# 128-row expert items with weight blocks stationary, in a one-core mixture-of-experts encoder

## What is computed

```python
def expert_block(args):                       # one block of up to 128 token rows of one expert
    e, tok, gt = args
    xb = hf[tok]
    g = xb @ w_gate[e] + b_gate[e]            # 1024 x 1024 each
    u = xb @ w_up[e] + b_up[e]
    g = jnp.minimum(g, SWIGLU_LIMIT)          # 7.0
    u = jnp.clip(u, -SWIGLU_LIMIT, SWIGLU_LIMIT)
    act = (u + 1.0) * (g * jax.nn.sigmoid(g * SWIGLU_ALPHA))
    y = act @ w_down[e] + b_down[e]
    return y * gt[:, None]
```

## Time and profile before

| | |
|---|---|
| median of 3 runs | 2243.87 us (2242.58 to 2245.83) |
| the profiled execution | 2242.51 us, its span 2240.7 us |
| granted TensorE clock, mean | 0.988 |
| busy share: TensorE, weight loads, VectorE, ScalarE, GpSimd | 97%, 45%, 29%, 25%, 20% |
| moved by DMA | 499.68 MB, 223 GB/s on average |

### The profile page before, as it was taken

One profiled execution on the slowest core, in us unless ns is written; L12 is line 12 of the kernel. 1 busy time (PEld: TensorE's weight loads), 2 busy tenths in 40 slices (PEclk: granted clock), 3 DMA queues, 4 the chain that ended last, 5 costly groups with the idle time before them and its releaser, 6 DMA issues.

```text
span 2240.7 us, 30792 instructions
## 1 busy us (share of the span) xinstructions
PE 2177.0 (97%) x10323; PEld 1006.9 (45%) x10324; DVE 649.7 (29%) x1915; ACT 564.8 (25%) x1160; POOL 457.1 (20%) x490
## 2 busy tenths in 40 slices
PE   8999999996999999999999899999999999999997
PEld 4444577543444344344434434434443444444443
DVE  2100599255322222221222212312112221222233
ACT  2000588211221222211122221222112221222223
POOL 1014011223121222212121221221122121122222
PEclk9999999997999999999999999999999999999998
DMA  7100200325567977758869795793889967677775
GB/s 265 44 35 0 116 1 1 110 105 199 187 204 288 364 249 239 284 188 316 312 205 365 237 367 192 238 351 121 326 303 381 348 234 277 247 253 262 255 262 188
DMA packets 149336, 499.68 MB, mean 223 GB/s; under 512 B 10265, under 2 KB 34478, under 8 KB 148750
## 3 DMA queue, kind: packets, MB, share of 16 engines
q1 hardware_dynamic: 113632, 443.80, 51.3%
q0 software_dynamic: 33792, 50.35, 10.9%
q10 hardware_dynamic: 1874, 5.02, 0.6%
HBM read 460.84 MB, written 42.50 MB: 225 GB/s over the span
## 4 chain that ended last, share of the span: by engine, by line
PE 94%; DMA 3%; DVE 1%; issue 1%; ACT 0%; POOL 0%; SPq 0%; DVEq 0%; ACTq 0%; POOLq 0%
PE psum L1530 41%; PE psum L1566 14%; PE psum L1264 10%; PE psum L1325 5%; PE psum L1577 4%; PE psum L1348 3%; PE psum L1314 3%; PE psum L1443 2%; PE psum L1538 2%; DMA weights<-in_w_down 2%; PE psum L1524 2%; PE psum L1512 1%; PE psum L1589 1%; PE psum L1601 1%; PE psum L1357 1%; DMA weights<-in_w_up 1%
## 5 line engine op out<-in xcount | busy, mean ns | idle before, releaser
L1530 PE MATMUL psum<-weights,work 128*128 128x512 f32 (+2 forms) x3008 | 968.3, 594 | 0.0
L1530 PEld LDWEIGHTS psum<-weights,work 128*128 128x128 f32 (+2 forms) x3008 | 364.9, 159 | 449.7 <-issue 443.7
L612 POOL DMA_INDIRECT residual_rows<-work x184 | 286.6, 1558 | 444.6 <-ACT work L818 398.2
L1566 PE MATMUL psum<-weights,work 128*128 128x512 f32 x768 | 337.5, 592 | 0.0
L1072 DVE TENSOR_REDUCE work<-psum 128x8 f32 x47 | 8.7, 184 | 790.0 <-PE psum L1457 790.0
L571 POOL DMA_INDIRECT work<-normed_rows,work x48 | 49.3, 1028 | 862.6 <-DVE work L1059 801.9
L1264 PE MATMUL psum<-weights 128*128 128x512 f32 x512 | 220.9, 592 | 1.3 <-DVE weights L890 1.3
L1566 PEld LDWEIGHTS psum<-weights,work 128*128 128x128 f32 x768 | 143.9, 190 | 164.4 <-issue 160.8
L790 ACT ACTIVATE work<-psum 128x256 f32<-128x256 f32 x188 | 71.9, 383 | 386.3 <-PE psum L1530 362.1
L777 ACT ACTIVATE work<-psum 128x512 f32<-128x512 f32 x96 | 57.6, 600 | 435.0 <-PE psum L1443 433.3
L1151 DVE TENSOR_SCALAR work<-psum 128x256 f32<-128x256 f32 x188 | 79.6, 424 | 259.6 <-ACT work L790 252.8
(11 more groups left out here) (213 smaller groups left out, 1669.2 us busy)
## 6 DMA issues: line engine op xcount, KB each, us to landing
weights<-in_w_gate SPq DMA_DIRECT2D x64, 2048.0 KB
weights<-in_w_up SPq DMA_DIRECT2D x64, 2048.0 KB
weights<-in_w_down SPq DMA_DIRECT2D x64, 2048.0 KB, 10.6
weights<-in_w_in SPq DMA_DIRECT2D x8, 768.0 KB, 14.4
residual_rows<-x SPq DMA_DIRECT2D x9, 512.0 KB, 5.4
normed_rows<-work ACTq DMA_DIRECT2D x9, 512.0 KB, 4.8
x<-in_x SPq DMA_DIRECT2D x8, 512.0 KB, 9.7
bias_rows_repeated<-bias_rows SPq DMA_DIRECT2D x4, 1024.0 KB, 9.9
```

The source lines that it names most:

```text
L612: pl.indirect_dma_start(acc_d[:, :], bass.IndirectOffsetOnAxis(dest[:, b:b + 1], 0), yrow[:, b * BLK:(b + 1) * BLK], None, compute_op=ALU. ...
L1530: mm = pe.matmul(out.rearrange("p (m n) -> p m n", m=2), xT[:, k, lo:lo + cols], wgu[:, :, k, blk * BLK:(blk + 1) * BLK], start=False, sto ...
L1566: mm = pe.matmul(bank(4 + h), actT[:, k, :], wdn[:, k, h * HALF:(h + 1) * HALF], start=False, stop=(k == DT - 1))
```

## The change

In 128-row items the sides are exchanged for gate and up: a 128x128 block of the weights is stationary and the 128 token rows move, so the result lies with inner columns on partitions, as the down projection needs it. The transposes and the copies' results are no longer used there: `down_all` takes `hid` itself. The bias products go; VectorE's unit, for every kind of item, adds a bias per partition from a new table `bias_cols` (loaded once, 16 columns an expert; the up half has one added by GpSimd; for the other kinds the table holds zeros, as their bias is still added on TensorE). The column is addressed from registers by the item's kind and expert. The sigmoid now reads the clamped gate from SBUF, and the clamps are in another order. In the 128-row body `hidden` is gone; ScalarE's copies stay and are released by steps on `s_htp` within the gate/up products and the down bias. Two sets of semaphores (`s_x`, `s_res`) become one.

```diff
@@ sync @@
             sp.wait_ge(s_biasp, 1)
+            sp.dma_start(bias_128, t["bias_cols"]).then_inc(s_bcols, 16)
             sp.dma_start(gfin, ...
@@ gpsimd @@
+                if i == 6:
+                    pl.wait_ge(s_biasp, 1)
+                    pl.memset(bias_none, 0.0).then_inc(s_bzero, 1)
...
             gather_rows(1)
+            pl.wait_ge(s_bcols, 16)
+            pl.tensor_scalar(up_cols, up_cols, 1.0, None, ALU.add).then_inc(s_bready, 1)
             pl.wait_ge(s_accin, 16 * (TT + 1))
@@ scalar @@
             def sigmoid(j, b):
-                act.wait_ge(s_gu, UNIT * j + b + 1)
-                act.activation(sig[:, b, :], bank(b, BLK), ACT.Sigmoid, scale=ALPHA).then_inc(s_sig, 1)
+                act.wait_ge(s_gcl, 2 * UNIT * j + (2 * b + 2))
+                act.activation(sig[:, b, :], gact[:, b, :], ACT.Sigmoid, scale=ALPHA).then_inc(s_sig, 1)
@@ vector @@
+            dve.wait_ge(s_bzero, 1)
+            dve.wait_ge(s_bready, 1)
+
+            def own_columns():
+                return (dve.snap(own_kind, min_val=0, max_val=KINDS - 1) * (16 * EXPERTS) +
+                        dve.snap(own_expert, min_val=0, max_val=EXPERTS - 1) * 16)
 
-            def unit(j, b):
+            def unit(j, b, cols):
+                dve.wait_ge(s_gu, UNIT * j + b + 1)
+                for s in range(2):
+                    dve.tensor_scalar(gact[:, b, s * P:(s + 1) * P], bank(b, P, s * P),
+                                      bias_cols[:, bass.ds(cols + (2 * b + s), 1)], LIMIT, ALU.add,
+                                      ALU.min).then_inc(s_gcl, 1)
+                for s in range(2):
+                    dve.tensor_scalar(ucl[:, b, s * P:(s + 1) * P], bank(b, P, BLK + s * P),
+                                      bias_cols[:, bass.ds(cols + (DT + 2 * b + s), 1)], LIMIT + 1.0, ALU.add,
+                                      ALU.min).then_inc(s_ucl, 1)
+                dve.wait_ge(s_gcl, 2 * UNIT * j + (2 * b + 2))
                 dve.wait_ge(s_sig, UNIT * j + b + 1)
-                dve.tensor_scalar(ucl[:, b, :], bank(b, BLK, BLK), LIMIT + 1.0, 1.0 - LIMIT, ALU.min,
-                                  ALU.max).then_inc(s_ucl, 1)
-                dve.tensor_tensor(gact[:, b, :], bank(b, BLK), sig[:, b, :], ALU.mult).then_inc(s_sg, 1)
-                dve.wait_ge(s_ucl, UNIT * j + b + 1)
+                dve.tensor_tensor(gact[:, b, :], gact[:, b, :], sig[:, b, :], ALU.mult).then_inc(s_sg, 1)
+                dve.wait_ge(s_ucl, 2 * UNIT * j + (2 * b + 2))
                 dve.wait_ge(s_sg, UNIT * j + b + 1)
-                dve.scalar_tensor_tensor(hid[:, b, :], gact[:, b, :], ACT_LIMIT, ucl[:, b, :], ALU.min,
+                dve.scalar_tensor_tensor(hid[:, b, :], ucl[:, b, :], 1.0 - LIMIT, gact[:, b, :], ALU.max,
                                          ALU.mult).then_inc(s_hid, 1)
@@ tensor @@
+                def gate_up_128(b, ks):
+                    for k in ks:
+                        for m in range(2):
+                            for s in range(2):
+                                mm = pe.matmul(bank(b, P, m * BLK + s * P), wgu[:, m, k, (2 * b + s) * P:(2 * b + s + 1) * P],
+                                               xT[:, k, :], start=(k == 0 and m + s == 0), stop=(k == DT - 1 and m + s == 2))
+                                if b and k == DT - 1 and m + s == 0:
+                                    mm.then_inc(s_htp, 1)
+                    return mm
...
                 def down_all(b):
-                    pe.wait_ge(s_aTm, UNIT * j + b + 2)
+                    pe.wait_ge(s_hid, UNIT * j + UNIT + b + 1)
...
-                            mm = pe.matmul(bank(4 + h), actT[:, k, :], wdn[:, k, h * HALF:(h + 1) * HALF],
+                            mm = pe.matmul(bank(4 + h), hid[:, b, (k - 2 * b) * P:(k - 2 * b + 1) * P], wdn[:, k, h * HALF:(h + 1) * HALF],
...
                 if tokens == 128:
-                    gate_up_ends(0)
-                    gate_up_ends(1)
-                    hidden(0)
-                    gate_up_ends(2)
-                    hidden(1)
-                    gate_up_ends(3)
+                    for b in range(4):
+                        gate_up_ends(b)
                     next_item()
-                    hidden(2)
                     rows(1)
                     down_bias()
                     down_all(0)
-                    hidden(3)
                     down_all(1).then_inc(s_d03, 1)
```

More of the change, by code:

```diff
@@ L202, in encoder_kernel @@
         bdn = biasp[0:3 * EXPERTS, 2 * D:3 * D]
+        bias_cols = Z[:, 12288:12288 + KINDS * EXPERTS * 16]
+        bias_128 = bias_cols[:, 0:EXPERTS * 16]
+        bias_none = bias_cols[:, EXPERTS * 16:]
+        up_cols = bias_128.rearrange("p (e m f) -> p e m f", m=2, f=DT)[:, :, 1, :]
         xg = Z[:, 0:1024]
@@ L325, in encoder_kernel @@
         s_ucl = sem("up_clamped")
+        s_gcl = sem("gate_clamped")
+        s_bcols = sem("bias_columns_in")
+        s_bzero = sem("bias_columns_cleared")
+        s_bready = sem("bias_columns_ready")
         s_sig = sem("sigmoid_ready")
@@ L1166, in chain @@
                         dve.wait_ge(s_dve, j * PER + (LOOP0 + local[0]))
-                    e1 = dve.value_load(items[0:1, bass.ds(j + 1, 1)], min_val=0, max_val=EXPERTS - 1)
+                    cols = own_columns()
+                    dve.reg_load(own_expert, items[0:1, bass.ds(j + 1, 1)])
+                    dve.reg_load(own_kind, items[0:1, bass.ds(j + (2 * TABLE + 1), 1)])
+                    e1 = dve.snap(own_expert, min_val=0, max_val=EXPERTS - 1)
                     e3 = dve.value_load(items[0:1, bass.ds(j + 3, 1)], min_val=0, max_val=EXPERTS - 1)
-                    kind = dve.value_load(items[0:1, bass.ds(j + (2 * TABLE + 1), 1)], min_val=0, max_val=KINDS - 1)
+                    kind = dve.snap(own_kind, min_val=0, max_val=KINDS - 1)
                     places(chain, j + 1, kind)
@@ L1176, in _ @@
                             index_parts(j + 2)
-                        unit(j, b)
+                        unit(j, b, cols)
                     dve.wait_ge(s_biased, j + 1)
@@ L1194, in _ @@
             dve.sem_inc(s_found, 1)
-            unit(last, 0)
-            unit(last, 1)
+            cols = own_columns()
+            unit(last, 0, cols)
+            unit(last, 1, cols)
             dve.wait_ge(s_added, n_items)
@@ L1201, in _ @@
             dve.sem_inc(s_dest, 1)
-            unit(last, 2)
-            unit(last, 3)
+            unit(last, 2, cols)
+            unit(last, 3, cols)
             dve.wait_ge(s_gfin, 16)
@@ L1517, in gate_up @@
                         return gate_up_32(b, ks)
-                    lo, cols, groups = (0, P, 1) if tokens == 128 else (0, 64, 2) if b < 2 and tokens > 32 else \
-                        (64 if b else 0, 32, 4)
+                    if tokens == 128:
+                        return gate_up_128(b, ks)
+                    lo, cols, groups = (0, 64, 2) if b < 2 else (64, 32, 4)
                     for c in range(groups):
-                        blk = b if tokens == 128 else 2 * c + b if cols == 64 else c
+                        blk = 2 * c + b if cols == 64 else c
                         out = PS[c * cols:(c + 1) * cols, b * HALF:(b + 1) * HALF].rearrange("p (m n) -> p m n", m=2)
@@ L1546, in down_bias @@
                                            start=True, stop=False)
+                            if h == 0:
+                                mm.then_inc(s_htp, 1)
                     if tokens in (64, 96):
@@ L1775 @@
     last = np.concatenate([gain, np.repeat(share.reshape(KINDS, -1), P, 0)], 1).astype(np.float32)
+    bias_cols = np.stack([inputs["b_gate"][0], inputs["b_up"][0]], 1).reshape(EXPERTS, 2, DT, P)
+    bias_cols = bias_cols.transpose(3, 0, 1, 2).reshape(P, EXPERTS * 16)
     arrays, aps = {}, {}
-    for name, a in list(inputs.items()) + [("onehot", onehot), ("edges", edges), ("tables", tables), ("same", same),
+    for name, a in list(inputs.items()) + [("onehot", onehot), ("edges", edges), ("tables", tables), ("same", same), ("bias_cols", bias_cols),
                                            ("last", last)]:
```

19 lines of the change are left out of this document (11 added, 8 removed).

## The result

| | before | after |
|---|---|---|
| median | 2244.70 us (4 runs, 2242.58 to 2245.83) | 2318.35 us (4 runs, 2317.03 to 2320.95) |
| ratio, 95% interval | | 1.0332 (1.0319 to 1.0344) |
| span of the profiled execution | 2240.7 us | 2319.0 us |
| granted TensorE clock, mean | 0.988 | 0.974 |
| busy share: TensorE, weight loads, VectorE | 97%, 45%, 29% | 94%, 60%, 34% |

A forecast was written before the change was run, and what follows sets the result against it. TensorE, 94% of the chain, was taken as the bound; -15.1 + 13.2 + 4.2 + 0.5 - 0.7 = +2.1 us on 2242.5, forecast 2245 us, no change. The range was 2230 to 2272.

The forecast's parts named there:

- The 128-row items on TensorE: 24 items: 42.2 us of bias products and transposes removed, 27.1 added by the exchange at 0.1117 us pitch; 15.1 us less.
- The rival of a pitch that doesn't hold: Gate/up products of 128-row items: 0.118 us a record over long runs, +39 us, 2284; chance 8%.
- VectorE's unit: All 47 items: the unit grows from 1.20 to 2.0 us (1.85 to 2.4), hidden in 128- and 96-row items.
- 32-row items: Choice of next expert comes later behind four longer units: 2.2 us in six of eight items, 13.2 us more.
- 64-row items: Down products start 0.6 us later behind a delayed sigmoid and ScalarE copy; seven items, 4.2 us more.
- The rival of hidden units: Small items hide the longer unit if it stays under 1.35 us: 2227 to 2230, faster; chance 14%.
- The start: Before the first item: bias table lands near 566, VectorE's loop begins near 567 instead of 563; 0.5 us more (0 to 1.5).
- The end: Last item: ScalarE's copy for block 3 no longer waits for the last transposes; 0.7 us less.
- the weighing of the code: Rival that TensorE's longer loop no longer stays loaded: 2253 to 2300, likeliest near 2256, slower; chance 32%.
- the prediction's own sign for it: TensorE's queue: instruction packets after 761 us, with idle time behind a jump that no semaphore explains.
- Eight such places at 1 us are +8: Lower case of refetched loop code: TensorE stalls behind short products of 96- and 32-row items, largely covered by queued products.
- The upper case of the rival: Refetched loop code: sixteen places with two fetches of 2 us, +60, within the code rival's 2253 to 2300.

The follow-up runs named there:

- wait_moved: Changed kernel with VectorE's waits for cleared columns and bias table moved behind the first item's count and index copies; 2314.55 us.
- two_units: Changed kernel with shared 64/96-row code, earlier expert choice, later table wait, and the new VectorE/ScalarE unit only in 128-row items; 2233.57 us, ratio to before 0.9945.
- order_128_last: Changed kernel with TensorE's code for the four kinds laid in the order 32, 64, 96, 128 instead of 32, 128, 64, 96; 2299.18 us.

## Why the prediction was wrong

**The 128-row items on TensorE: right.** The pitch was put at 0.1117 us and is 0.1116; the gain was put at 0.63 us an item and is 0.58 on average. The rival of a pitch that doesn't hold is out, which leaves the row of attention a good witness for runs eight times as long. The rule of the Trainium skill, TensorE: Matmul & The Clock Gate, section Back-to-back issue gap (81 ns a pair where the product alone needs 56), applied as a ratio, would have made it 0.16; the trace disagrees with that use of it.

**VectorE's unit: right in place and size.** It was put at 2.0 us; in a 32-row item of the changed kernel the copies that begin two units in a row start 2.03 us apart:

```profile
856.89 0.60 DVE L1176 TENSOR_SCALAR work<-psum,work 128x128 f32<-128x128 f32 x2
...
858.92 0.60 DVE L1176 TENSOR_SCALAR work<-psum,work 128x128 f32<-128x128 f32 x2
...
861.52 0.37 PE L1555 MATMUL psum<-work,weights 128*128 128x128 f32 x1 [1.14 <-DVE work L1096]
```

TensorE waits 1.14 us for L1096, the choice, as forecast. 32-row items grew by 1.94 us (forecast 2.2 in six of the eight), 64-row items by 0.70 where undisturbed (forecast 0.6). The rival of hidden units falls with that. That a 128-wide operation takes 0.28 us was too short: those rows read and write `weights`, and the new ones, which read PSUM, take 0.346 on average. But their successors start 0.26 apart, against 0.27 in the prediction, and the unit came out right.

**The start: wrong by some 2 us.** "VectorE's loop may begin near 567 instead of 563 ... I count 0.5 us more" took the first index products at 569.2 as the next thing wanted, and did not list what is queued behind the new wait on VectorE: the count. That step is due for every added wait. The first item grew by 5.4 us where the prediction has 0.5 and 2.2; what stood behind the wait is 2.4 of it (wait_moved), against the 0.5.

**The end: right**, 0.7 us less: the last item begins 79.0 us later and the span is 78.3 us longer.

**The step that failed is the weighing of the code.** The sum has no term for the longer loop: it puts its cost at nothing. The mechanism was there as a rival, with its place, its evidence and the prediction's own sign for it, instruction packets after 761 us and idle time behind a jump. It got 32% and 2256 us; it cost 52.9 us of idle time and, with the clock behind it, some 15 more. The second figure is the remainder of the 79.0 us by which the last item begins later, not a measured one: 52.9 in the stalls, 5.4 + 0.4 in and ahead of the first item, 13.6 in 32-row and 4.9 in 64-row items at 1.94 and 0.70 each, less 23 x 0.58 = 13.4, make 63.8, and 15.2 are left. Two things were misjudged.

*The chance.* "The trace shows only that seven stay loaded" held the whole answer in one more step. Seven loads after 540 us, and the packet in which the loop starts, are eight. The runs agree with eight as far as they go: loops of 1676 to 1768 instructions fit, one of 1818 does not. If a store holds eight packets of some 260, one of them must then go to code outside the loop, likely to what stands behind it; no run shows this by itself. The Trainium skill, Runtime: NRT & Kernel Launch, section Instruction fetch mechanics, gives 128 KiB in blocks of 16 KiB, which is eight, and 2048 instructions. Set beside the number of instructions it would have misled: the changed loop has 2032, fewer than that, and does not fit. The section speaks of a stall when a branch leaves a window of two pages; the trace disagrees for TensorE, whose loop of 1676 instructions ran from 761 us to its end without a packet. A page and a row that named the same number of packets were treated as two weak hints, instead of one strong one, and "no row shows a limit" was taken as evidence against one.

*The price.* "At least 1.8 us, what a load of 28 KB takes to land, and up to some 4 under traffic" was taken from a data load. The branches show 3.2 to 4.2 us for the shorter kind and 5.9 to 7.6 for the longer. The packets themselves are the smaller part of this: in the branch of 774.6 us both lie between 2.6 and 5.5 us after its start. What fills the rest the profile does not show. "Eight such places at 1 us are +8" supposed that the queued products cover most of it. Behind the 64 short down products of a 96-row item they covered nothing visible: 6.64 us of idle time for a branch of 6.87. The upper case of the rival, "+60", was the right one, and was called less likely with no row for that. That it comes so near is in part luck: it supposed sixteen places with two fetches of 2 us, and the trace has 13 places with one or two fetches and 0.4 to 6.9 us of idle time each.

## What to carry to other kernels

Count the instructions of a loop on the engine that bounds it, before and after, and set the count against what its instruction queue loads once and then no more. A loop that just fits is a cliff and not a slope: 82 instructions more cost nothing here and 142 cost 60 us, though none of them is ever executed. When an edit is right for one kind of work and shares its code with others, give it to that kind alone: two_units keeps the gain of the 128-row items, 13.5 us in all, and pays 3.1 us of it in the 96-row items and 0.8 in the first.

## What the runs showed that was not expected

- A jump to code that is not loaded takes 5.9 to 7.6 us in most cases, three to four times the landing time of 28 KB of data, and two such jumps in a row 13.5 us.
- Leaving the last packet of a loop that is too long does not always cost: order_128_last has 24 such items and 20 long branches in all, with 33.5 us of idle time.
- A stall of 6.8 us is followed by a stretch at 1.2 GHz, and 16 products that took 3.44 us before took 5.02 there.
- The place of code ahead of a loop matters as well: with the first item's code 663 instructions away from the dispatch, the jump to it cost 6 to 7 us, once in the execution.
